# Splitting the constant and parameter loads in two, and loading one activation table with Ln and Exp by hand, in a two-layer hybrid diffusion step

## What is computed

```python
ada = jax.nn.silu(cond) @ p['ada_w'] + p['ada_b']
sh_m, sc_m, g_m, sh_f, sc_f, g_f = jnp.split(ada[:, None, :], 6, axis=-1)
hm = rms_norm(x, p['norm_mix_w']) * (1.0 + sc_m) + sh_m
m, st = token_mixer(hm, p, cache)
x = x + g_m * m
hf = rms_norm(x, p['norm_ffn_w']) * (1.0 + sc_f) + sh_f
x = x + g_f * hier_moe(hf, p)
```

## Time and profile before

| what | us |
|---|---|
| median of three runs | 1420.52 |
| lowest and highest of them | 1415.59, 1420.88 |
| span of the profiled execution, first to last instruction | 1411.4 |

### The profile page before, as it was taken

The page is one execution under the profiler, slowest core; times in us unless marked ns, Lnnn a source line. Parts: engine busy times, 40 slices in busy tenths (PEclk is TensorE's granted clock), DMA queues, the critical chain, the costliest instruction groups (busy, mean ns, idle before and its releaser), DMA issues.

```text
span 1411.4 us, 18228 instructions
## 1 busy us (share of the span) xinstructions
PE 1236.9 (88%) x7508; PEld 968.0 (69%) x7508; DVE 678.2 (48%) x857; ACT 491.7 (35%) x550; POOL 86.5 (6%) x93
## 2 busy tenths in 40 slices
PE   4689678998679999999967996798886999999997
PEld 3489568797656666666664985687776666666665
DVE  0255535443355556656423654445424556566652
ACT  2234521112244444444213444111322544444440
POOL 0000203130000000000000011222100000000000
PEclk8799879999789999999988997899996999999999
DMA  9744600121508888888865354102060488888960
GB/s 389 337 179 179 242 9 31 35 90 44 225 0 336 338 338 339 346 345 336 343 269 244 146 199 172 34 31 94 1 243 26 179 345 335 335 340 344 354 268 32
DMA packets 15195, 299.00 MB, mean 212 GB/s; under 512 B 1920, under 2 KB 1920, under 8 KB 2176
## 3 DMA queue, kind: packets, MB, share of 16 engines
q1 hardware_dynamic: 14688, 296.67, 53.5%
q0 software_dynamic: 416, 1.05, 0.2%
HBM read 295.61 MB, written 2.10 MB: 211 GB/s over the span
## 4 chain that ended last, share of the span: by engine, by line
PE 79%; DVE 6%; issue 5%; ACT 5%; DMA 3%; POOL 1%; SPq 0%; DVEq 0%; POOLq 0%; ACTq 0%
PE ps L824 16%; PE ps L795 8%; PE ps L796 8%; PE ps L797 8%; PE ps L713 4%; PE ps L483 3%; PE ps L485 3%; PE ps L484 3%; PE ps L663 3%; PE ps L638 3%; PE ps L659 3%; DMA param<-in_param 3%; PE ps L459 2%; PE ps L838 1%; PE ps L862 1%
## 5 line engine op out<-in xcount | busy, mean ns | idle before, releaser
L1602 DVE TENSOR_TENSOR ring_r<-ring,arena_r 128x2048 fp32r<-128x2048 f32 x124 | 284.3, 2292 | 129.5 <-ACT arena_r L1127 129.5
L1127 ACT ACTIVATE arena_r<-ring 128x2048 fp32r<-128x2048 f32 x124 | 236.7, 1909 | 231.2 <-PE ps L797 231.2
L795 PE MATMUL ps<-arena_r 128*128 128x512 f32 x512 | 231.3, 452 | 5.4 <-DVE ring_r L1602 3.5
L824 PE MATMUL ps<-ring,arena 128*128 128x512 f32 x512 | 230.3, 592 | 1.0 <-DVE arena L1608 1.0
L797 PE MATMUL ps<-ring_r,arena_r 128*128 128x512 f32 x512 | 202.5, 395 | 0.0
L796 PE MATMUL ps<-arena_r 128*128 128x512 f32 x512 | 202.3, 395 | 0.0
L824 PEld LDWEIGHTS ps<-ring,arena 128*128 128x128 f32 x512 | 96.8, 189 | 99.0 <-issue 91.9
L795 PEld LDWEIGHTS ps<-arena_r 128*128 128x128 f32 x512 | 96.3, 188 | 38.9 <-issue 16.7
L483 PE MATMUL ps<-arena_r 128*128 128x256 f32 x384 | 109.7, 286 | 10.4 <-DVE ring_r L1256 10.4
L796 PEld LDWEIGHTS ps<-arena_r 128*128 128x128 f32 x512 | 96.6, 189 | 31.8 <-issue 14.4
L797 PEld LDWEIGHTS ps<-ring_r,arena_r 128*128 128x128 f32 x512 | 96.0, 188 | 22.6
(11 more groups left out here) (301 smaller groups left out, 1548.9 us busy)
## 6 DMA issues: line engine op xcount, KB each, us to landing
ring<-in_moe SPq DMA_DIRECT2D x64, 3072.0 KB, 10.1
ring<-in_ada_w SPq DMA_DIRECT2D x16, 3072.0 KB, 11.1
ring<-in_w_feat SPq DMA_DIRECT2D x8, 3072.0 KB, 14.1
ring<-in_w_tok SPq DMA_DIRECT2D x2, 2112.0 KB, 24.0
ring<-in_w_out SPq DMA_DIRECT2D x2, 2048.0 KB, 7.3
ring<-in_w_out SPq DMA_DIRECT2D x4, 1024.0 KB, 4.9
param<-in_param SPq DMA_DIRECT2D x2, 1501.5 KB, 23.4
const<-in_const SPq DMA_DIRECT2D x1, 1899.0 KB, 16.6
```

What stands on the lines that cost most here:

```text
L795: mm(out, x_hi, hi[:, k], start=k == 0, stop=False)
L824: done = mm(bank(4 + half), act_t[:, i % 2, kk * P:(kk + 1) * P], ring[i % RING][:, at:at + 512], start=i == 0 and kk == 0, stop=i == PER_ ...
L1127: go(w_hi[:, 0:4096].rearrange("p (w n) -> p w n", w=2)[:, :, cols], ring[j][:, 0:4096].rearrange("p (w n) -> p w n", w=2)[:, :, cols], AC ...
L1602: tt(low_w, raw_w, high_w, ALU.subtract).then_inc(sem[name], 1)
```

## The change

- `const` is laid out with `zeros`, `ones` and `fold` in front, and loaded in two parts: 268 columns right behind `xT`, and the other 3530 behind `w_tok` (a new semaphore, `const_late`).
- `param` is loaded in two parts: the 443 columns ahead of `nat_bias` right behind the first part of `const`, and the other 2560 behind the rest of `const` (`param_late`). For the second layer the 443 columns are issued in the first, once routing is done (`route_dve`), ahead of the loop that refills the experts' slots; the 2560 columns go where the whole went.
- The addition to `nat_bias` moves from the start of DVE's layer to behind `unit_low(6)`; PE, DVE, ACT and POOL wait for the late parts where they first use them.
- Three loads of a table set that holds both Ln and Exp are written by hand: after the first Silu, after the Silu of the convolution, and at the end of a layer.
- Semaphores of the two branches of the mixture are shared, which frees five, and takes two increments off PE, one off ACT and two off DVE per layer.

```diff
-    ("ident", P), ("zeros", P), ("ones", P), ("blockones", P), ("upto_f", P), ("upto_b", P), 
+    ("zeros", P), ("ones", P), ("fold", 2 * ADA_TILES), ("ident", P), ("blockones", P), ("upto_f", P), ("upto_b", P),
...
+CONST_FIRST = CONST["fold"].stop
+PARAM_FIRST = PARAM["nat_bias"].start
+LOG_EXP_SET = "natural_log_exp_and_others"
...
                         sp.dma_start(xT[:], src["xT"]).then_inc(const_in, 16)
-                        sp.dma_start(const[:], src["const"]).then_inc(const_in, 16)
+                        sp.dma_start(const[:, 0:CONST_FIRST], src["const"][:, 0:CONST_FIRST]).then_inc(const_in, 16)
+                        sp.dma_start(param[:, 0:PARAM_FIRST], src["param"][0][:, 0:PARAM_FIRST]).then_inc(sem["param_dma"], 16)
                     if i == RING - 1:
 
-                        if l > 0:
+                        if l == 0:
+                            sp.dma_start(const[:, CONST_FIRST:], src["const"][:, CONST_FIRST:]).then_inc(const_late, 16)
+                        else:
                             sp.wait_ge(sem["layer_done"], l + 1)
-                        sp.dma_start(param[:], src["param"][l]).then_inc(sem["param_dma"], 16)
+                        sp.dma_start(param[:, PARAM_FIRST:], src["param"][l][:, PARAM_FIRST:]).then_inc(sem["param_late"], 16)
...
+                if l + 1 < DEPTH:
+                    sp.wait_ge(sem["route_dve"], rise(l, "route_dve", 1))
+                    sp.dma_start(param[:, 0:PARAM_FIRST], src["param"][l + 1][:, 0:PARAM_FIRST]).then_inc(sem["param_dma"], 16)
...
+                pe.wait_ge(const_late, 16)
                 pe.wait_ge(sem["proj_act"], rise(l, "proj_act", 10))
...
+                pe.wait_ge(sem["param_late"], rise(l, "param_late", 16))
                 pe.wait_ge(sem["pad_act"], rise(l, "pad_act", 1))
...
-                    for name, n in (("cb_mm", 16), ("gate_mm", 32), ("up_mm", 32)):
-                        pe.sem_inc(sem[name], n)
+                    pe.sem_inc(sem["cb_mm"], 16)
...
             go(condp[:, :, 2 * (ADA_TILES - 1):2 * ADA_TILES], condT, ACT.Silu).then_inc(cond_e, 1)
+            nc.scalar.preload_act_table_set(LOG_EXP_SET)
...
                 go(A("qkv"), A("qkv"), ACT.Silu).then_inc(sem["silu_act"], 1)
+                nc.scalar.preload_act_table_set(LOG_EXP_SET)
...
+                act.wait_ge(const_late, 16)
                 act.wait_ge(sem["gates_dve"], rise(l, "gates_dve", 1))
...
                         act.sem_inc(sem[name], PER[name])
+                nc.scalar.preload_act_table_set(LOG_EXP_SET)
...
                 dve.wait_ge(sem["param_dma"], rise(l, "param_dma", 16))
-                tt(Q("nat_bias").rearrange("p (a c) -> p a c", c=GRID_W), Q("nat_bias").rearrange("p (a c) -> p a c", c=GRID_W),
-                          bc(C("colmask").unsqueeze(1), 2 * HEADS, GRID_W), ALU.add).then_inc(chain_dve, 1)
-                dve.wait_ge(chain_dve, links.next())
...
                 unit_low(6)
+
+                dve.wait_ge(const_late, 16)
+                dve.wait_ge(sem["param_late"], rise(l, "param_late", 16))
+                tt(Q("nat_bias").rearrange("p (a c) -> p a c", c=GRID_W), Q("nat_bias").rearrange("p (a c) -> p a c", c=GRID_W),
+                          bc(C("colmask").unsqueeze(1), 2 * HEADS, GRID_W), ALU.add).then_inc(chain_dve, 1)
+                dve.wait_ge(chain_dve, links.next())
```

More of the change, by code:

```diff
@@ L197, in build_trunk @@
         const_in = ctx.enter_context(nc.semaphore("const_in"))
+        const_late = ctx.enter_context(nc.semaphore("const_late"))
         cond_in = ctx.enter_context(nc.semaphore("cond_in"))
@@ L797, in gate_up @@
                         last = mm(out, x_hi, lo[:, k], start=False, stop=k == KT - 1)
-                    last.then_inc(sem["half_mm" if first_half else "gu_mm"], 1)
+                    last.then_inc(sem["gate_mm" if first_half else "up_mm"], 1)
                 def gathered_step(e, i, turn, last=False):
@@ L897, in _ @@
                         step(e, e % RING, last=e == N_EXPERTS - 1)
-                    for name in ("ga_mm", "cg_mm", "st_mm", "half_mm", "gu_mm", "tr_mm", "scatter_mm"):
+                    for name in ("ga_mm", "cg_mm", "st_mm", "tr_mm", "scatter_mm"):
                         pe.sem_inc(sem[name], PER[name])
@@ L1132, in gathered_step @@
                     if ahead > 1:
-                        high_half(e + 2, (i + 2) % RING, "hi_a", "half_mm", 0)
+                        high_half(e + 2, (i + 2) % RING, "hi_a", "gate_mm", 0)
                     if ahead > 0:
-                        act.wait_ge(sem["gu_mm"], rise(l, "gu_mm", e + 2))
-                        go(g_silu[:, (i + 1) % 2], bank((i + 1) % 2, FF), ACT.Silu).then_inc(sem["g_silu"], 1)
+                        act.wait_ge(sem["up_mm"], rise(l, "up_mm", e + 2))
+                        go(g_silu[:, (i + 1) % 2], bank((i + 1) % 2, FF), ACT.Silu).then_inc(sem["silu"], 1)
                     if ahead > 1:
-                        high_half(e + 2, (i + 2) % RING, "hi_b", "gu_mm", 1)
+                        high_half(e + 2, (i + 2) % RING, "hi_b", "up_mm", 1)
                     if i == PER_GROUP - 1:
@@ L1178, in _ @@
                         step(e, e % RING, ahead=N_EXPERTS - 1 - e)
-                    for name in ("ga_hi", "st_act", "hi_a", "hi_b", "g_silu", "yg_hi"):
+                    for name in ("ga_hi", "st_act", "hi_a", "hi_b", "yg_hi"):
                         act.sem_inc(sem[name], PER[name])
+                nc.scalar.preload_act_table_set(LOG_EXP_SET)
         @block.vector
@@ L1607, in gathered_step @@
                         dve.wait_ge(sem["tr_mm"], rise(l, "tr_mm", e + 1))
-                        copy(act_t[:, i % 2], bank(2 + i % 2, FF)).then_inc(sem["act_t"], 1)
+                        copy(act_t[:, i % 2], bank(2 + i % 2, FF)).then_inc(sem["act_dve"], 1)
                     if ahead > 1:
@@ L1675, in _ @@
                     residual(40, range(KT)).then_inc(sem["layer_done"], 1)
-                    for name in ("sel", "ht_lo", "ga_lo", "cg_dve", "lo_a", "lo_b", "g_act", "act_t", "yg_lo"):
+                    for name in ("sel", "ht_lo", "ga_lo", "cg_dve", "lo_a", "lo_b", "yg_lo"):
                         dve.sem_inc(sem[name], PER[name])
```

21 lines of the change are left out of this document (10 added, 11 removed).

## The result

| what | before | changed |
|---|---|---|
| median, us | 1419.64 (4 runs, 1415.59 to 1420.88) | 1386.47 (4 runs, 1384.85 to 1390.52) |
| ratio to before, over the runs | | 0.9777, interval 0.9757 to 0.9797 |
| profiled execution: span, us | 1411.4 | 1384.1 |

The medians lie 33.2 us apart, and by the ratio the change is worth 2.2%. The sign was forecast, the size was not: 1398.6 was the number and 1390 the lower end of the range.

What follows compares the result with a forecast made beforehand. PE's work, 79% of the chain of waits, bounds the kernel; gains lie where PE stands. Start 10.8, tables 10.8 and turn 0.3 make 21.9 us off 1420.52: 1398.6 us, range 1390 to 1405.

Steps and rivals of the forecast that it cites:

- The start: Loads at the kernel's start: split const and param let PE's projection begin at 41.5 us, 10.8 us earlier.
- the third product: PE's third ada_w product at the start: begins at 31.0 us instead of 34.73, taking 5.05 us.
- The bounds, 7.2 and 13.0: Gain at the start: 7.2 us if small pieces cost what they spare, 13.0 if PE's third product takes 2.83.
- The small pieces: Split const and param loads at the start: priced by bytes; by the skill's table the gain would be 8.5 us.
- `nat_bias`: DVE's addition moved behind unit_low(6): 0.69 us hidden in idle time, costing nothing, or 1.4 us in two layers without cover.
- the late parts: Rest of const and param: landed by 43.5 us, asked for by DVE at about 102, so no cost.
- the turn: Change to the second layer: PE's 8.61 us gap stays within 1 us, with 0.3 us won.
- The rival in which it pays: Turn to the second layer: a shorter param transfer returns 3 to 7 us, say 1394 us; chance 0.12.
- The tables: Table loads at the norms: eight between Ln and Exp at 1.30 us plus four times 0.1, together 10.8 us.
- the rival where the queue takes some back: Costly small pieces, or one or two more PE stretches at 1.2 GHz: 1402 to 1408, say 1404 us; chance 0.14.
- a load is worth more than its row: Each table load removed also frees an engine drain of 1.38 us, 11.0 us more: 1387.6 us; chance 0.03.
- 9.1 us from span to median: Distance of the runs' median above the profiled span of 1411.4 us, carried over unchanged to the forecast time.

Runs made afterwards that it cites:

- extra_loads: The changed kernel with a table load put back between Ln and Exp at four norms in both layers, eight loads: 1406.82 us.
- after_again: The changed kernel itself, run once more beside the follow-up kernels on the same chip: 1387.11 us, 0.9795 of before.
- start_only: The changed kernel without its three hand-written table loads, so the compiler places loads ahead of each Ln and Exp again: 1407.15 us.
- pe_unrolled: The changed kernel with PE's program written out for both layers in place of the loop: 1381.82 us.
- fill_all_unrolled: The changed kernel with 15 unread PE products per layer, 7 more each ahead of L544 and L852, and PE's program written out: 1350.49 us.

## Why the prediction fell short

**The start: right.** ACT's first square was forecast for about 15 us and came at 14.60; the third product for 31.0, came at 30.94; `w_feat` for 50.9, came at 50.83 (as the end of ACT's wait). The projection started at 39.92 and not at 41.5. Of the 1.6 us, 1.2 stand ahead of the column product, at 35.02 instead of 36.2, mostly since the third product took 4.15 where I kept 5.05; the rest are 4.9 us of short steps where I had 5.3. The bounds, 7.2 and 13.0, hold 12.4. The small pieces cost their bytes. The table of the Trainium skill (DMA: Bandwidth & Descriptors, Measured), which is of transfers issued from GpSimd and by which the gain would have been an estimated 8.5 us, does not fit the third product at 30.94. In the runs the start was worth 9.6 or 12.1, around the forecast 10.8.

**`nat_bias`, the late parts, the turn: right.** DVE did the addition at 99.10 without waiting for a DMA; I had said near 101. The turn kept its gap, 8.84 us. The rival in which it pays is out.

**The tables: the step that failed.** "Between a Ln and its Exp the load costs its own time and nothing more", and so 4 x 2 x 1.30 = 10.4 us plus 0.4. As far as DVE goes, it holds: DVE's idle time fell by 10.8 us. What failed is that the sum stopped where the wait reaches PE. PE's wait was priced at its length, as though PE behind it went on as fast as before. It doesn't. Behind such waits PE runs at 1.2 GHz for a stretch (0.50 in the router's product), and with waits 1.28 us longer or shorter these stretches change or lie elsewhere: between `extra_loads` and `after_again` by 0.9 us behind the norm of keys and queries, by 0.9 in L727, by nothing in the router's product, and by 2.0 in the inverse, far from any load. How long a stretch gets and where it begins, these rows don't tell. Measured, this term is 17.5 to 20.0 us instead of 10.8. I had the fact in hand (the third product's 5.05 us and a window at 0.50, "every start of PE after a gap here is slow") and used it only as a danger, in the rival where the queue takes some back. That rival had the sign wrong: taking waits away gave stretches back.

**The rival "a load is worth more than its row": right in size, wrong in cause.** It gave 1387.6, against 1386.47, and had a chance of 0.03. Its drain is not there. The rows that spoke against it spoke against the drain only, and I let them stand against the price as well.

**What is left.** Start and tables by these runs come to 27 us taken each alone, 30 taken together (1416.70 to 1387.11); the first pair of medians had 33.2. The medians of before alone lie between 1416.7 and 1421.0 from one set of runs to the next, and its runs between 1412 and 1423 within one. I had carried over 9.1 us from span to median as though they lay around the span. They don't: in each run whose span and time both stand, the time is some 1.8 us above the span, which puts the profiled execution of before at some 1413, one of its shortest runs. From the medians the difference is 33.2, from the two spans 27.3. In the profiles, `start_only` leads the kernel before by 13.6 us at the turn (as PE's first product of the second layer) and by only 5.8 at the end. Half of what it loses, 4.0 us, goes in the DeltaNet's inverse of the second layer, the rest in smaller pieces from the first product of the projection to L727. In that inverse the kernel before, in its profile, has no slow stretch behind the wait of 2.35 us (L659 is L673 of the changed kernel; timeline of 950 to 1000 us):

```profile
977.98 1.14 PE L659 MATMUL ps<-arena 128*128 128x128 f32 x8
```

That the runs of before differ by which of these stretches fall out long is a reading of these two traces, and wasn't tested by itself.

## What to carry to other kernels

A wait of PE is priced at its length and at what the matmuls behind it take at the lower clock; read the granted clock just behind each wait before a saving or a cost is put into a sum, look for it far downstream as well, and ask whether PE would have waited behind the slow matmuls anyway. Where such waits can't be removed, products that nobody reads, a little shorter than the wait, can pay: here 1.0% on top of the change with 15 a layer, and 2.6% with 29 and a program written out. And a span is set against runs by the distance that the runs themselves show between span and time, not by the distance to a median.

## What was not expected of the hardware

- Work added to PE made the kernel faster: 15 fp32 products of 0.88 us per layer, 26 us of PE time in all, gave 14 us.
- The price of a wait has steps: eight copies that move the Exp by 1.17 us cost 12.6 us (and 8 to 21 from run to run), eight that move it by 1.29 cost 21 with a narrow spread, 1405.5 to 1409.2.
- The lower clock can come later than the wait and stay into work that is dense: in `extra_loads` the first eight matmuls behind the wait of 2.35 us still took 1.15 us, the next eight, behind another wait of 0.57, 2.07, and those from 277 to 281, without a gap, up to 2.06. In `after_again`, behind the same wait, it fell on the first 16 (a granted clock of 0.55 over them) and was over with them. Why it fell differently behind equal waits isn't told by these rows.
- PE's program written out without the jump at the turn removed the 8.84 us. In `pe_unrolled` PE then stood twice in straight code, 3.58 and 1.92 us, put down to issue; in `fill_all_unrolled`, written out the same way, only 0.25.
